# Reordered filler matmuls in two attention stages, the first expert pass of TensorE outside its loop, and its first gate/up half on the first copied half of the rows

## What is computed

```python
def trunk_layer(x, ...):
    h = rmsnorm(x, p['norm1']) * (1 + sc1) + sh1          # sh, sc, g: from silu(cond) @ w_ada
    q, k, v, gq, gk, gv, gg, lr_f, lr_b, ga, gb = _split_proj(jnp.matmul(h, p['w_in']))
    o_attn = block_attention(q * HEAD_DIM ** -0.5, k_all, v_all)
    o_gla, s_f, s_b = bidirectional_gla(gq, gk, gv, la_f, la_b, s0_f, s0_b)
    o_gla = rmsnorm(o_gla, p['gla_norm']) * jax.nn.silu(gg)
    merged = sigmoid(ga) * (o_attn @ p['w_pa']) + sigmoid(gb) * (o_gla @ p['w_pb'])
    x = x + g1 * jnp.matmul(merged, p['w_out'])
    h2 = rmsnorm(x, p['norm2']) * (1 + sc2) + sh2
    return x + g2 * grouped_moe(h2, ...)                  # 16 experts, top 2 of the best group
```

## Time and profile before

| | us |
|---|---|
| median of 3 runs | 1016.98 |
| lowest, highest of them | 1016.48, 1020.95 |
| profiled execution, its time | 1015.12 |
| its span, first to last instruction | 1013.1 |

### The profile page before, as it was taken

The page is one execution under the profiler, slowest core; times in us unless marked ns, Lnnn a source line. Parts: engine busy times, 40 slices in busy tenths (PEclk is TensorE's granted clock), DMA queues, the critical chain, the costliest instruction groups (busy, mean ns, idle before and its releaser), DMA issues.

```text
span 1013.1 us, 13671 instructions
## 1 busy us (share of the span) xinstructions
PE 966.3 (95%) x4910; PEld 565.5 (56%) x4910; DVE 389.2 (38%) x1011; ACT 238.1 (23%) x521; POOL 99.9 (10%) x85
## 2 busy tenths in 40 slices
PE   9999999989989999999899999899899999999987
PEld 3458876677845443443344688766786444344333
DVE  4099513972261222222351421258535222222124
ACT  2213223430123222221130312335101222122212
POOL 0000004731100000000000000066210000000000
PEclk9999999999999999999999999999999999999999
DMA  9999462814999999999998523255277999999992
GB/s 389 388 399 410 180 245 96 323 43 184 407 351 412 418 421 369 423 421 422 425 426 351 206 95 155 83 223 193 95 298 284 405 408 423 422 373 421 422 421 103
DMA packets 37378, 317.48 MB, mean 313 GB/s; under 512 B 4280, under 2 KB 4432, under 8 KB 5328
## 3 DMA queue, kind: packets, MB, share of 16 engines
q1 hardware_dynamic: 36144, 311.28, 75.6%
q0 software_dynamic: 1184, 5.53, 1.3%
HBM read 314.93 MB, written 1.86 MB: 313 GB/s over the span
## 4 chain that ended last, share of the span: by engine, by line
PE 79%; DMA 13%; DVE 4%; ACT 2%; issue 1%; SPq 0%; ACTq 0%; DVEq 0%
PE ps L1054 18%; DMA ring<-w_gu 12%; PE ps L594 11%; PE ps L1066 7%; PE ps L748 7%; PE ps L943 5%; PE ps L1012 3%; PE ps L861 3%; PE ps L929 3%; PE ps L607 3%; PE ps L766 3%; PE ps L574 1%; PE ps L1027 1%; DMA ring<-w_ada 1%; PE ps L704 1%; PE ps L713 1%
## 5 line engine op out<-in xcount | busy, mean ns | idle before, releaser
L1054 PE MATMUL ps<-ring,tmq 128*64 128x512 f32 x928 | 214.1, 602 | 15.2 <-DMA ring<-w_gu 11.7
L1054 PEld LDWEIGHTS ps<-ring,tmq 128*64 128x64 f32 x928 | 68.1, 139 | 141.6 <-issue 124.4
L594 PE MATMUL ps<-more,ring 128*128 128x256 f32 x512 | 114.3, 381 | 0.5 <-ACT more L1123 0.5
L1066 PE MATMUL ps<-ring,tmq 128*64 128x512 f32 x512 | 113.8, 596 | 0.0
L594 PEld LDWEIGHTS ps<-more,ring 128*128 128x128 f32 x512 | 96.1, 190 | 15.5 <-issue 2.5
L1887 DVE TENSOR_TENSOR tmq<-tmq,ps 128x256 f32<-128x256 f32 x32 | 13.5, 421 | 204.4 <-ACT tmq L1378 204.4
L1123 ACT ACTIVATE tmq<-ps 128x256 f32<-128x256 f32 (+3 forms) x124 | 55.6, 462 | 149.2 <-PE ps L748 62.8
L1066 PEld LDWEIGHTS ps<-ring,tmq 128*64 128x64 f32 x512 | 35.1, 137 | 65.8 <-issue 62.4
L748 PE MATMUL ps<-ring,more 128*128 128x512 f32 (+1 forms) x192 | 69.9, 523 | 0.0
L1898 DVE SCALAR_TENSOR_TENSOR x<-ps,mod,x 128x128 f32<-128x128 f32 x256 | 67.6, 342 | 2.0 <-PE ps L1012 1.9
L1378 ACT ACTIVATE tmq<-ps 128x256 f32<-128x256 f32 x32 | 12.3, 383 | 224.5 <-PE ps L1054 224.5
(11 more groups left out here) (256 smaller groups left out, 1040.9 us busy)
## 6 DMA issues: line engine op xcount, KB each, us to landing
ring<-w_gu SPq DMA_DIRECT2D x116, 1024.0 KB, 13.8
ring<-w_down SPq DMA_DIRECT2D x64, 1024.0 KB, 12.4
ring<-w_ada SPq DMA_DIRECT2D x24, 2048.0 KB, 9.3
ring<-w_in SPq DMA_DIRECT2D x14, 2048.0 KB, 18.0
ring<-w_out SPq DMA_DIRECT2D x4, 2048.0 KB, 8.1
more<-w_gu SPq DMA_DIRECT2D x8, 1024.0 KB, 14.3
cst<-consts SPq DMA_DIRECT2D x2, 2080.0 KB, 16.7
ring<-w_in SPq DMA_DIRECT2D x4, 1024.0 KB, 23.9
```

The costliest lines, as they stand in the source:

```text
L594: mm = pe.matmul(ps[:, 5, i * NT:(i + 1) * NT], w[:, k, m * P:(m + 1) * P], h[:, k, :], start=k == 0, stop=k == KT - 1)
L1054: mm = pe.matmul(ps[r:r + SLOTS, half, :].rearrange("p (j n) -> p j n", j=2), hg[:, k, e, 0:SLOTS], gu_unit(l, kh, e, in_more)[:, part, :, ...
L1066: mm = pe.matmul(ps[r:r + SLOTS, 2 + n, :], at_[:, k, r:r + SLOTS], down_unit(l, k // 2)[:, e, k % 2, n * 512:(n + 1) * 512], start=k == 0 ...
```

## The change

It touches the programs of TensorE, ACT and DVE; SP's and POOL's are as before.

1. Attention: in each of the eight blocks the gate chunk is cut. 14 (stream 0) or 13 (stream 1) of its 16 matmuls stay ahead of the wait for the normed probabilities; the other 2 or 3 come after the transposes, ahead of the wait for ACT's copy. ACT's copy of the gate chunk moves behind its copy of the transposed probabilities. The wait for `att_o_copied` after the last block moves from before `gla_in(0)` into `gla_keys(0)`.
2. End of GLA: the transposes of stream 0 go ahead of `gla_out(7)` and into PSUM bank 0 (stream 1: bank 1) and so does ACT's copy of them. The last pa chunk is cut: its first 4 matmuls stay where the chunk was, the second 4 come after `gla_out(7)`. They and the first modulation unit of `front` come ahead of the transposes of stream 1. DVE merges pa chunk 3 after it has normed stream 1.
3. Experts: the first pass stands outside the loop, its waits against constants; TensorE loads the number of passes only after it, and further passes stand behind `If(passes - 1)` as a second copy of the code. The first gate/up half of pair 0 waits for the first of ACT's two copies, the second half for the second one. ACT adds its 3 to `m_hg` only after TensorE's first gate/up group is complete.

```diff
@@ TensorE
-            def gate_chunk(l, c):
+            def gate_chunk(l, c, first=0, last=2 * KT):
...
+            def pa_half(l, m, i):
...
-                for i in range(2):
-                    for k in range(4):
-                        mm = pe.matmul(ps[:, 5, i * NT:(i + 1) * NT], w[:, k, (2 * m + i) * P:(2 * m + i + 1) * P],
-                                       ot[:, k, :], start=k == 0, stop=k == 3)
-                mm.then_inc(pa_mm, 1)
+                pa_half(l, m, 0)
+                if m < 3:
+                    pa_half(l, m, 1)
@@ attention block
-                        fill(l)
+                        flush()
+                        kind, chunk = fills.pop(0)
+                        kept = 2 * KT - 2 - s
+                        gate_chunk(l, chunk, 0, kept)
                         pe.wait_ge(normed, b + 1)
...
                         mm.then_inc(prob_t, 1)
+                        gate_chunk(l, chunk, kept)
                         pe.wait_ge(prob_copied, b + 1)
...
-                pe.wait_ge(att_o_copied, 4 * (l + 1))
                 pe.wait_ge(la_ready, 2 * (l + 1))
@@ end of GLA
+                def turn_o(s):
+
+                    pe.wait_ge(g_exp, 8 * (l + 1))
+                    pe.wait_ge(g_normed, 2 * l + s + 1)
+                    for k in range(4):
+                        mm = pe.transpose(ps[:, s, k * P:(k + 1) * P], tm[:, s, k * P:(k + 1) * P], ident)
+                    mm.then_inc(g_nt, 1)
...
                     fill(l)
+                    if i == 7:
+                        turn_o(0)
                     gla_out(i)
-                while fills:
-                    fill(l)
-                flush()
-                pe.wait_ge(pa_used, 4 * (l + 1))
-                pe.wait_ge(g_exp, 8 * (l + 1))
-                pe.wait_ge(g_o_copied, 8 * (l + 1))
-                for s in range(S):
...
+                pa_half(l, 3, 1)
+                pre, post = front(l), tail(l)
+                for w in pre[:1]:
+                    ada_a(*w)
+                turn_o(1)
@@ experts
-                passes = pe.snap(pe.value_load(npass[0:1, l:l + 1], min_val=1, max_val=4))
...
-                        if kh == 0:
+                        if opening:
+                            pe.wait_ge(m_hg[l], kh + 1)
+                        elif kh == 0:
                             pe.wait_ge(m_hg[l], q * 4 + 5)
...
-                with pe.Fori(0, passes) as pss:
-                    expert_pair(pss, 0, first=True)
+                def one_pass(pss, opening=False):
+
+                    expert_pair(pss, 0, first=True, opening=opening)
...
+                one_pass(0, opening=True)
+                passes = pe.snap(pe.value_load(npass[0:1, l:l + 1], min_val=1, max_val=4))
+                with pe.If(passes - 1):
+                    with pe.Fori(1, passes) as pss:
+                        one_pass(pss)
@@ ScalarE
-                        fill(l)
                         act.wait_ge(prob_t, b + 1)
...
                              ps[:, 2:2 + nb, :]).then_inc(prob_copied, 1)
+                        fill(l)
...
-                act.sem_inc(m_hg[l], 3)
...
+                act.wait_ge(m_gu[l][0], 2)
+                act.sem_inc(m_hg[l], 3)
                 with act.Fori(0, passes) as pss:
@@ VectorE
-                fill(l)
                 gla_norm(1)
                 for hh in range(GH):
                     ins = gla_scale(1, hh)
                 ins.then_inc(g_normed, 1)
-                while fills or late:
-                    fill(l)
+                merge_a(l, 3)
```

More of the change, by code:

```diff
@@ L584, in ada_b @@
                 mm.then_inc(ada_cols, 1)
-            def gate_chunk(l, c):
-                w = full(l, "gates", c // 2)
-                if l or c:
-                    pe.wait_ge(gate_exp, l * 8 + c)
-                for i in range(2):
-                    m = (c % 2) * 2 + i
[L593 to L596, removed]
+            def gate_chunk(l, c, first=0, last=2 * KT):
+                w = unit((l, "gates", c // 2))[0]
+                if first == 0:
+                    full(l, "gates", c // 2)
+                    if l or c:
+                        pe.wait_ge(gate_exp, l * 8 + c)
+                for j in range(first, last):
+                    i, k = j // KT, j % KT
+                    m = (c % 2) * 2 + i
+                    mm = pe.matmul(ps[:, 5, i * NT:(i + 1) * NT], w[:, k, m * P:(m + 1) * P], h[:, k, :],
+                                   start=k == 0, stop=k == KT - 1)
+                if last == 2 * KT:
+                    mm.then_inc(gate_mm, 1)
+            def pa_half(l, m, i):
+                w = unit((l, "pa", 0))[0]
+                for k in range(4):
+                    mm = pe.matmul(ps[:, 5, i * NT:(i + 1) * NT], w[:, k, (2 * m + i) * P:(2 * m + i + 1) * P],
+                                   ot[:, k, :], start=k == 0, stop=k == 3)
+                if i:
+                    mm.then_inc(pa_mm, 1)
             def pa_chunk(l, m):
-                w = full(l, "pa", 0)
+                full(l, "pa", 0)
                 if m == 0:
@@ L915, in _ @@
                           stop=True).then_inc(g_nt, 1)
-                flush()
-                pre, post = front(l), tail(l)
-                for w in pre[:1]:
-                    ada_a(*w)
                 w = full(l, "pb", 0)
@@ L1029, in sort_rows, with expert_pair @@
                             mm.then_inc(m_rowmm[l], 1)
-                def expert_pair(pss, pr, in_more=False, later=False, first=False):
+                def expert_pair(pss, pr, in_more=False, later=False, first=False, opening=False):
                     q = pss * PAIRS + pr
@@ L1305, in _ @@
                         inv_root(GLA_RMS, RSQ * l + 3)
-                fill(l)
                 inv_root(GLA_RMS, RSQ * l + 4)
-                while fills:
-                    fill(l)
-                for s in range(S):
-                    act.wait_ge(g_nt, CS_ROWS + 3 * l + s + 1)
-                    copy(ogt[:, :, s * T:(s + 1) * T],
-                         ps[:, 4 + s, :].rearrange("p (a n) -> p a n", a=4)).then_inc(g_nt_copied, 1)
+                turned(1)
                 act.wait_ge(g_nt, CS_ROWS + 3 * l + 3)
@@ L1532, in fill @@
                         late.append((l, n))
-                    elif kind == "pa":
+                    elif kind == "pa" and n < 3:
                         merge_a(l, n)
```

17 lines of the change are left out of this document (9 added, 8 removed).

## The result

The changed kernel takes 1007.37 us (median of 4 runs, 1006.50 to 1007.99); the kernel before, run beside it, 1018.74 (4 runs, 1016.48 to 1020.95). The ratio is 0.9888, with a 95% interval of 0.9859 to 0.9917: 1.1% faster, where 1.5% was forecast, and 0.37 us above the range. The profiled executions stand 7.2 us apart: 1015.12 us before and 1007.88 after, spans 1013.1 and 1005.9.

The account below looks back on a forecast made before the run. TensorE bounds the kernel until about 250 us in layer 0, then mostly the weight stream. Gains 9.2 + 3.4 + 1.0 + 1.95 - 0.7 = 14.85 us off 1015.12 give 1000.27, or 1002.1 as median; range 998.5 to 1007.0.

Parts of the forecast that it names:

- The regimes: Until about 250 us in layer 0 TensorE sets the pace; then the weight stream does, so earlier savings carry one for one.
- Part 1: Attention: moved gate matmuls cover ACT's copy of the probabilities; 4.6 us a layer, 9.2 in all, bounds 7.9 to 9.6.
- the covers of two and three gate matmuls: Attention blocks: three gate matmuls fill 1.3 us and two fill 0.9, both just covering ACT's copy.
- the softmax rival: Attention: a wait on the normed probabilities replaces the removed one; half of part 1 lost, 1006.7 us, chance 0.10.
- Part 2: End of GLA: reordered work starts w_pb 3.4 us earlier in layer 0 and 1.0 us in layer 1.
- The clock stayed up, as taken: End of GLA, layer 0: clock assumed to stay up as the 1.62 us wait shrinks; a fall gives back 1.7 us.
- Part 3's opening: Start of the experts: TensorE's register load leaves the path; 1.05 us in layer 0, 0.9 in layer 1.
- the new code at the end of the pass: Layer boundary: register load and taken branch, priced at SP's 0.5 us, lose 0.7 us once; bounds nothing to 3.9.
- the upper bound, an 8 KB transfer of 3.7 us: Layer boundary: branch priced as a transfer running just as expert loads start, in place of SP's 0.5; 3.9 us lost.
- the jump costs a fetch: Layer boundary rival: the branch over the skipped pass forces an instruction fetch; 3.9 us instead of 0.7, 1005.3 us, chance 0.24.
- the rival that transfers absorb the start of the experts: Start of the experts: transfers absorb 1.95 us, and GLA's clock falls anyway, 1.7 us; 1005.8 us, joint chance 0.09.
- the rival of the luckier clock: Last gate/up half: the clock stays up there, 1.6 us less; 1000.5 us, chance 0.07.

Follow-up runs that it names:

- part 1 alone: The kernel before with only the attention edits (gate chunks cut, ACT's copies reordered, wait for the attention output moved): 1010.40 us, ratio 0.9909.
- part 3 alone: The kernel before with only the experts edits (first pass outside the loop, later register load, branch, first half on first copy): 1022.57 us, ratio 1.0041.

## Why the prediction missed

**Right.** The regimes: layer 0's attention and GLA moved the whole stream of weights, and 8.0 us were in hand at its end. *Part 1*, forecast 4.6 a layer, measured 4.3; the covers of two and three gate matmuls are needed, since with one alone the wait comes back in all eight blocks. The total is inside the bounds (7.9 for both layers; measured 8.7), and the softmax rival fell: no wait for the normed probabilities is among TensorE's waits. *Part 2*: 3.5 and 1.1, forecast 3.4 and 1.0; but of the 3.5 only 1.9 are the change's. The timeline of the end of GLA in layer 0 shows each step as written:

```profile
217.07 1.89 PE L605 MATMUL ps<-more,ring 128*128 128x256 f32 x8
218.80 0.60 PE L912 MATMUL ps<-cst,tmq 128*128 128x128 f32 x4
219.28 0.49 PE L899 MATMUL ps<-tmq,st 128*128 128x128 f32 x2
...
219.83 1.89 PE L605 MATMUL ps<-more,ring 128*128 128x256 f32 x8
221.66 1.92 PE L574 MATMUL ps<-ring,cs 128*32 128x512 f32 x16
223.51 0.66 PE L912 MATMUL ps<-cst,tmq 128*128 128x128 f32 x4
...
224.94 2.40 PE L944 MATMUL ps<-more,ring 128*128 128x256 f32 x10 [0.46 <-ACT lrt L1146]
```

Transposes of stream 0, product, pa, modulation unit, transposes of stream 1, w_pb, with no idle time but the last 0.46 us, and the unit at its 1.9 us. The clock stayed up, as taken, but the reason given for it (the wait of 1.62 us shrinks) is not borne out: with that wait in place it stayed up too, in part 1 alone and in part 3 alone. So this 1.6 us is luck: it measures a fall that one of three executions with those waits had. None of the eleven with part 2 has it, so the change may make it rarer, which is not shown. *Part 3's opening*: 1.2 and 1.0, forecast 1.05 and 0.9, and for the reason given (the register load leaves the path, the increments stay).

**Wrong: the term "the new code at the end of the pass"**, 0.7 us lost, measured 8.0. It was the branch's wait for its code that was mis-sized. The price of the branch was SP's 0.5 us, "the only taken If in the trace"; it was 6.09. The load and the lead of the sequencer came out a little better than worked out: the branch starts 0.4 us before the scatter ends (507.6 against 504.30 + 3.72), where the working had it 0.1 us after. Of its 6.09 us, 5.75 stand open. The remaining 2.3 us were in no term and in no rival: the clock falls to half during the wait (at 511.7, with the engine idle since 508.0), and the norm sums behind it run at 6.05 instead of 3.75 us. Even the upper bound, an 8 KB transfer of 3.7 us at this place, was under the fetch, so the rival "the jump costs a fetch" had the right mechanism with the wrong price: 3.9 for 8.0. The fetch itself is in the trace: the packet waits 3.6 us, moves for 1.1, and 1.4 us later the branch ends. With 8.0 the sum is 15.55 - 8.0 = 7.6 us, and 1015.12 - 7.6 = 1007.6, beside the 1007.88 profiled; how near that is, is in part luck, as said of the two clock falls. The choice between two rows was made by the wrong likeness: SP's branch is like it in kind, but the distance decides, and I had written that SP's skipped code is shorter. The prediction quoted the rule of the Trainium skill ("Runtime: NRT & Kernel Launch", "Instruction fetch mechanics": a taken branch to a target outside the two pages held forces a fetch). The runs agree with it. A page there is 16 KiB or 256 instructions, the profile's instruction packets are of 0.57 MB / 35 = 16 KB, and the step lies between 260 skipped instructions and 560, that is between one page and a little over two.

**The smaller misses.** 9.0 us were forecast at the last gate/up matmul of layer 0, 8.0 arrived: 0.6 less from a later start of the attention itself (108.66 before, 109.28 after; TensorE waits 1.2 us for modulation weights ahead of it), 0.3 less from attention, 0.3 more from GLA and the opening. At the first expert matmul 8.5 were in hand, at the start of the last pair 8.1. Whether the stream of weights took the difference (the rival that transfers absorb the start of the experts) is not shown: with three pairs skipped, and with both halves waited for, the lead grew over the same stretch, by 0.2 and 0.35 us.

**Luck in layer 1.** Its 7.3 us look like more than the 6.5 of the terms (4.6 + 1.0 + 0.9). The timelines give 4.3 + 1.1 + 1.0 = 6.4 up to the first expert matmul and 5.6 at the start of the last pair. Then the last pair's gate/up matmuls gain 1.7 us, because the kernel before had a clock fall at 983.2 in its profiled execution and the changed kernel had its own at 948.6, ahead of that pair. That is the rival of the luckier clock, and it came true here as luck, not as an effect of the change: of the 14 profiled executions in this document ten have the fall in this pair, and the changed kernel's is one of the four without.

**The medians** differ by 11.4 us where the profiles differ by 7.2. The kernel before ran between 1016.48 and 1020.95 in these runs and was profiled at 1015.12. Much of this spread goes with the clock. Among its 13 runs beside the first experiments, those of 1015.13 and 1015.75 us had a mean granted clock of 0.997, that of 1021.16 us one of 0.989. In the traces each execution has one to three clock falls of 3.41 us at changing places, each worth up to 1.7 us, besides those noted below.

**Not tried:** whether the same code laid out so that the usual path falls through, with the second pass placed out of line, would avoid the fetch; and whether a filler behind the branch keeps the clock up.

## What to carry to other kernels

Peeling one iteration out of a loop leaves a second copy of its body to jump over, and the jump is the price: count the instructions skipped before using any other branch of the trace as its measure, and look for what stands still if the fetch meets a full DMA stream. The page's instruction queue tells whether it happened: here three packets more, one of them within each branch. A loop's start-up cost can be moved instead (here eight semaphore increments ahead of a wait, 1.0 us a layer, for nothing). A wait of several microseconds on TensorE is to be priced with the slower clock that came with it: here 2.3 us on top of 5.8. And a slow stretch in one profiled execution is not a gain to be had until a second execution shows it too: 1.6 us of this forecast were such a stretch.

## What the runs showed of the hardware

- A taken branch of TensorE over 45 and 260 instructions: 0.21 and 0.33 to 0.35 us. Over 560 to 1170 (six kernels): 6.0 to 6.3 us beside a full stream of weights (421 to 425 GB/s), 3.3 to 3.8 us without one. Within each of these stands one instruction packet of 16 KB, which starts 3.5 to 3.8 us into the branch beside the stream and 0.9 to 1.0 us without it.
- All six kernels with such a long branch show the clock at 1.2 GHz for 6.83 us in layer 0, from 3.0 to 4.2 us after the start of the branch (511.7 to 518.5 in the changed kernel); none of the other eight has a fall at the layer boundary. The falls elsewhere last 3.41 us, but for the one at the very end of each execution and one of 6.83 in layer 1 of part 1 alone, at 716.3, within a wait of 1.6 us for DVE. The same wait in layer 0 brought none, in this kernel as in part 3 alone.
- Where idle time was put down to ACT's copy (0.67 us ahead of the first expert matmul), moving TensorE's increments removed all of it. Sequencer and ACT ended within a tenth of a microsecond of each other, and the profile names only one.
